# One-hots of the gate spreading: the first of each pair moved from VectorE and ScalarE to GpSimd

## The reference, cut to what matters

```python
best, sel = lax.top_k(cand, TOPK)
experts = jnp.take_along_axis(cand_idx, sel, axis=-1)
g = jax.nn.softmax(best, axis=-1).astype(tb.dtype)
act = jax.nn.gelu(jnp.einsum('td,thkd->thk', tb, u[experts]), approximate=False)
return jnp.einsum('thk,thkd->td', g * act, v[experts])
```

## Time and profile before

| | |
|---|---|
| median of 3 runs | 2717.73 us (2707.57 to 2720.52) |
| the profiled execution's own time | 2710.97 us |
| its span in the profile | 2709.1 us |
| its mean granted clock of TensorE | 0.979 |
| busy: PE, PEld | 2546.0 us (94%), 2100.2 us (78%) |
| busy: DVE, ACT, POOL | 1420.7 us (52%), 458.0 us (17%), 669.8 us (25%) |
| moved by DMA | 903.23 MB |

### The profile page before, as it was taken

The page is one execution under the profiler, slowest core; times in us unless marked ns, Lnnn a source line. Parts: engine busy times, 40 slices in busy tenths (PEclk is TensorE's granted clock), DMA queues, the critical chain, the costliest instruction groups (busy, mean ns, idle before and its releaser), DMA issues. The chain is left out here.

```text
span 2709.1 us, 40606 instructions
## 1 busy us (share of the span) xinstructions
PE 2546.0 (94%) x16083; PEld 2100.2 (78%) x16083; DVE 1420.7 (52%) x3161; ACT 458.0 (17%) x1371; POOL 669.8 (25%) x651
## 2 busy tenths in 40 slices
PE   8889987799899999999999999998999999999998
PEld 5564463346499999999999866464999999899997
DVE  2430020122279989985555321223799899855554
ACT  3220020012021125430000010121111254300000
POOL 0005000000004336563333000000043365633330
PEclk9799998999999999999999999999999999999999
DMA  7789969996928999999999896949089999999996
GB/s 244 239 280 295 350 246 386 407 362 248 407 85 315 382 353 396 402 384 410 409 409 409 295 378 223 379 162 368 1 339 376 350 397 401 385 409 409 409 409 226
DMA packets 254618, 903.23 MB, mean 333 GB/s; under 512 B 28522, under 2 KB 35850, under 8 KB 243631
## 3 DMA queue, kind: packets, MB, share of 16 engines
q1 hardware_dynamic: 170254, 608.05, 59.9%
q0 software_dynamic: 84176, 292.59, 28.0%
HBM read 880.10 MB, written 109.08 MB: 365 GB/s over the span
## 5 line engine op out<-in xcount | busy, mean ns | idle before, releaser
L2999 PE MATMUL ps<-xT,front 128*128 128x176 f32 x4096 | 645.1, 315 | 11.5 <-DMA front<-in_peer_uT 11.1
L2999 PEld LDWEIGHTS ps<-xT,front 128*128 128x128 f32 x4096 | 611.6, 190 | 29.5 <-DMA front<-in_peer_uT 28.2
L3032 PE MATMUL ps<-p1e_S,p_qT 128*128 128x192 f32 x2048 | 337.4, 327 | 6.5 <-DMA p_qT<-in_peer_v 6.5
L3032 PE MATMUL ps<-p0e_S,p_qT 128*128 128x192 f32 x2048 | 337.1, 327 | 4.8 <-DMA p_qT<-in_peer_v 4.8
L3032 PEld LDWEIGHTS ps<-p1e_S,p_qT 128*128 128x128 f32 x2048 | 332.4, 190 | 10.9 <-DMA p_qT<-in_peer_v 10.9
L3032 PEld LDWEIGHTS ps<-p0e_S,p_qT 128*128 128x128 f32 x2048 | 332.4, 190 | 8.9 <-DMA p_qT<-in_peer_v 8.6
L2735 DVE CUSTOM_DVE_ANT_0 front<-front,x_tok 128x1024 f32<-128x1024 f32 x256 | 308.6, 1218 | 10.2 <-DMA front<-in_peer_u,p1e_expert 4.1
L2636 POOL DMA_INDIRECT front<-in_peer_u,p0e_expert x128 | 158.3, 1237 | 340.8 <-DVE p0e_expert L2798 165.9
L2636 POOL DMA_INDIRECT front<-in_peer_u,p1e_expert x128 | 158.2, 1236 | 340.4 <-DVE p1e_expert L2798 163.8
L2745 DVE SCALAR_TENSOR_TENSOR h_tok<-front,p0e_dots,h_tok 128x1024 f32<-128x1024 f32 x127 | 163.1, 1284 | 145.6 <-DMA front<-in_peer_v,p0e_expert 144.8
L2745 DVE SCALAR_TENSOR_TENSOR h_tok<-front,p1e_dots,h_tok 128x1024 f32<-128x1024 f32 x127 | 163.1, 1284 | 144.0 <-DMA front<-in_peer_v,p1e_expert 143.2
(11 more groups left out here) (494 smaller groups left out, 2985.4 us busy)
## 6 DMA issues: line engine op xcount, KB each, us to landing
front<-in_peer_uT SPq DMA_DIRECT2D x256, 512.0 KB, 7.3
p_qT<-in_peer_v SPq DMA_DIRECT2D x256, 512.0 KB, 7.3
out_swa_sample<-in_cache_swa_w SPq DMA_DIRECT2D x32, 2040.0 KB, 23.8
e_ring<-in_mla_pages SPq DMA_DIRECT2D x84, 272.0 KB, 4.7
e_ring<-in_swa_kT SPq DMA_DIRECT2D x16, 1024.0 KB, 9.6
e_arena<-in_swa_v SPq DMA_DIRECT2D x16, 1024.0 KB, 14.3
out_swa_sample<-in_cache_swa_w SPq DMA_DIRECT2D x8, 2016.0 KB, 31.7
e_ring<-in_attn_w_in SPq DMA_DIRECT2D x6, 2048.0 KB, 35.1
```

The costliest lines, as they stand in the source:

```text
L2999: mm = pe.matmul(k.ps[:, SB[i % len(SB)], 0:TU], ur[:, i % NU, c, :], k.xT[:, c, D0:D0 + TU], start=(c == 0), stop=(c == KC - 1))
L3032: return pe.matmul(k.ps[:, c // 2, c % 2 * TD:(c % 2 + 1) * TD], vr[:, i % NV, c * P:(c + 1) * P], S[:, i, :], start=False, stop=(i == STE ...
```

## The change

GpSimd makes hotI, and puts the gate in at once: for each token of a group one `tensor_scalar` of 128x128 compares `iota` with the key (a scalar per partition) and multiplies by the gate (a second one). VectorE makes hotJ only; ScalarE's `gate_hots` is gone. GpSimd does the four instructions of group G ahead of gather `rows_behind_hots(G)`, five gathers further than VectorE's row at that point of its order; groups 0 and 1 both stand ahead of gather 62. The semaphore `keys_ready` is folded into `act_ready`, whose counts move up by two.

```diff
+    ROWS_AHEAD = 57
...
+        def rows_behind_hots(G):
+            return ROWS_AHEAD + sum(1 + i % 2 for i in range(FIRST - 1, SPLIT[max(G, 1) - 1] - 1)) + 5
...
         @block.gpsimd
         def _(pool):
+            def first_hots(G):
+                if G == 0:
+                    pool.wait_ge(act_ready, 5)
+                if G >= 2:
+                    pool.wait_ge(spread, G - 1)
+                if G == MORE_GROUP:
+                    pool.wait_ge(hot_ready, MORE_GROUP + 1)
+                for m in range(TG):
+                    t = TG * G + m
+                    last = pool.tensor_scalar(out=hotI[:, G % 2, m, :], in0=iota[:, :], scalar1=T3[:, 0, t:t + 1],
+                                              scalar2=T3[:, 2, t:t + 1], op0=ALU.is_equal, op1=ALU.mult)
+                last.then_inc(hot_turned, 1)
...
+                while G < GROUPS and rows_behind_hots(G) == n:
+                    first_hots(G)
+                    G += 1
                 if n >= NG:
                     pool.wait_ge(rows_used, n - NG + 1)
...
-                for hot, a in ((hotI, 0), (hotJ, 1)):
-                    dve.tensor_tensor(out=hot[:, G % 2, :, :], in0=iota[:, :].unsqueeze(1).to_broadcast([P, TG, P]),
-                                      in1=T3[:, a, t0:t0 + TG].unsqueeze(2).to_broadcast([P, TG, P]),
-                                      op=ALU.is_equal).then_inc(hot_ready, 1)
+                dve.tensor_tensor(out=hotJ[:, G % 2, :, :], in0=iota[:, :].unsqueeze(1).to_broadcast([P, TG, P]),
+                                  in1=T3[:, 1, t0:t0 + TG].unsqueeze(2).to_broadcast([P, TG, P]),
+                                  op=ALU.is_equal).then_inc(hot_ready, 1)
...
-            def gate_hots(G):
-                t0 = TG * G
-                act.wait_ge(hot_ready, 2 * G + 1)
-                for m in range(TG):
-                    last = act.activation(hotI[:, G % 2, m, :], hotI[:, G % 2, m, :], ACT.Copy,
-                                          scale=T3[:, 2, t0 + m:t0 + m + 1])
-                last.then_inc(hot_gated, 1)
...
-                pe.wait_ge(hot_ready, 2 * G + 2)
-                pe.wait_ge(hot_gated, G + 1)
+                pe.wait_ge(hot_ready, G + 1)
+                pe.wait_ge(hot_turned, G + 1)
```

More of the change, by code:

```diff
@@ L2518, in peer @@
         diff_ready, gated = k.sem(name + "_diff"), k.sem(name + "_gated")
-        turned, keys_ready = k.sem(name + "_turned"), k.sem(name + "_keys_ready")
+        turned, hot_turned = k.sem(name + "_turned"), k.sem(name + "_hot_turned")
         u_landed = [k.sem(f"{name}_u_landed{s}") for s in range(NU)]
@@ L2522, in peer @@
         dotted, gelu_done = k.sem(name + "_dotted"), k.sem(name + "_gelu")
-        hot_ready, hot_gated, spread = k.sem(name + "_hot"), k.sem(name + "_hot_gated"), k.sem(name + "_spread")
+        hot_ready, spread = k.sem(name + "_hot"), k.sem(name + "_spread")
         gate_copied, weight_ready, scaled = k.sem(name + "_copied"), k.sem(name + "_weight"), k.sem(name + "_scaled")
@@ L2597, in _ @@
                 if i == MORE_GELU_AT + NU:
-                    sp.wait_ge(act_ready, 4)
+                    sp.wait_ge(act_ready, 6)
                     sp.dma_start(carried[0:MORE, :], more_dots[:, :]).then_inc(more_landed, 16)
@@ L2625, in _ @@
         def _(pool):
+            def first_hots(G):
[10 more added lines that the diff above has]
+                last.then_inc(hot_turned, 1)
             pool.wait_ge(chosen, 1)
+            G = 0
             for n in range(ROWS):
@@ L2639, in _ @@
                 ).then_inc(row_landed[n % NG], 16)
+            assert G == GROUPS
         @block.vector
@@ L2783, in row @@
                     if col == 0:
-                        dve.wait_ge(act_ready, 5)
+                        dve.wait_ge(act_ready, 7)
                         link(dve.tensor_tensor(out=dots[:, :], in0=dots[:, :], in1=IJ[:, 0, 2, :], op=ALU.mult))
@@ L2815, in _ @@
             row()
-            dve.wait_ge(keys_ready, 2)
+            assert n_rows == ROWS_AHEAD
+            dve.wait_ge(act_ready, 5)
             one_hots(0)
@@ L2906, in take_keys @@
                                    k.ps[:, i, 0:3 * P].rearrange("p (a t) -> p a t", a=3)[:, :, 0:n],
-                                   ACT.Copy).then_inc(keys_ready, 1)
+                                   ACT.Copy).then_inc(act_ready, 1)
             before.root(act, 0)
@@ L2937, in _ @@
                 gelu(i)
-                if i == TURN_AT:
-                    gate_hots(0)
                 while G < groups_by(i):
@@ L2942, in _ @@
                     G += 1
-                    if G < GROUPS:
-                        gate_hots(G)
                 if i == MORE_GELU_AT:
```

## The result

The changed kernel takes 3037.38 us (median of 4 runs, 3033.85 to 3041.80) against 2716.89: a ratio of 1.118, 95% interval 1.116 to 1.120. That is 320 us slower, where 135 were forecast and the range ended at +237. The direction and the engine were right, the size was not.

The account below looks back on a forecast made before the run. VectorE was taken as full, with TensorE and the transfers level; afterwards GpSimd sets the pace. 46 groups x (5.34 - 3.87) = 67.6 us per layer, 135 for two, on 2717.7 gives 2853 us; range 2718 to 2955.

Parts of the forecast that it names:

- The bound: Gate spreading: three engines and the transfers level; what the stretch gains or loses goes to the end, once per layer.
- What goes: Per group VectorE loses one of two one-hots, 0.60 us, and ScalarE four gate multiplications of 0.390 us.
- The start's 2 us: Start of the spreading: three quick GpSimd steps fewer before the first spreading weights load may give 2 us.
- the rival in which GpSimd keeps up: Spreading: short tensor_scalars slip in and gathers wait less; gain about 10 to 14 us, 2704 to 2708; chance 0.17.
- What comes: Four new GpSimd tensor_scalars per group, priced from copies at 0.40 us each, bounds 0.28 and 0.55.
- the same sum: GpSimd's work plus waits per spreading group: 3.84 + 2.95 x 2.70/T, giving 5.34 us.
- T: New group period in the spreading, forecast at 5.34 us against 3.87 before.
- the sum of the upper bound: Spreading group with tensor_scalars of 0.55 and waits of 1.22: T = 4.44 + 4.81 x 2.70/T = 6.45, +237 us.
- The shared access: Spreading: GpSimd reads wait for VectorE instructions with two SBUF inputs, 0.41 or 0.60 us each times their share.
- Who waits: Spreading: GpSimd's gathers come late, VectorE waits for rows, TensorE for the weights and scalings behind them.
- VectorE and the clock: Spreading: VectorE not the bound at 4.87 us; rival, TensorE's clock falls, +343 us at the lower level, chance 0.04.

Follow-up runs that it names:

- v0_left_out: Changed kernel with GpSimd's four tensor_scalars and the first one-hot left out, only the semaphore raised: 2715.93 us, ratio 0.9994 to the kernel before.
- c2: Changed kernel with VectorE's row product replaced by a sum with one SBUF input: 2864.19 us.
- c1: Kernel before the change, with row products replaced by plain sums with one SBUF input: 2716.12 us.
- d1: Changed kernel with GpSimd's one-hots four gathers earlier in its order: 3001.39 us.
- the four kernels: Changed kernel with GpSimd's tensor_scalar at half the columns, compare only, constants for scalars, or two products: 2934.82, 2930.50, 2897.78, 2903.60 us.

## Why the prediction was wrong

- *The bound.* Right: three engines and the transfers level, the stretch going to the end once per layer, nothing made up later. The loss is 160 and 161 us.
- *What goes.* The start's 2 us and the 10 to 14 us of the rival in which GpSimd keeps up were too much: v0_left_out shows no gain (by its interval some 4 us at most).
- *What comes: the failed step.* "I take 0.40 us, between them, the copy being the nearer kind", with 0.55 as upper bound: it measured 0.79 us alone. The copy has no compare (0.35 us of it) and reads no scalars. With 0.79 in the same sum, T = 5.40 + 2.95 x 2.70/T = 6.6 us, or +252 us; this one term makes 117 of the 185 us missing. With 0.79 in the sum of the upper bound T is 7.20 us and the loss 306 us, so the measured 7.13 lies within it: the range failed by this price.
- *The shared access.* Its existence and the need for two SBUF inputs held (c2). Its size was low: 0.28 us per tensor_scalar was in the sum ((0.41 + 3 x 0.60) x 0.506/4), 0.47 is the mean, at a share of only 2.70/7.13 = 0.38: 1.24 us times the share, where the sum had 0.55 on average and the upper bound 1.02. Several waits in one instruction, which the bound left out, would explain that; they are not shown. The Trainium skill's rule (SBUF — State Buffer, Who interferes with whom) held for the tensor_scalars (mean 1.26 us beside row products, 0.82 beside sums with one input); that gathers wait too, c1's timeline shows again, 1.75 us behind one-hots for 0.94.
- *Who waits.* Wrong in place: VectorE stands before gates, TensorE before one-hots, not VectorE before rows. It would be rows with another order (d1).
- *VectorE and the clock.* VectorE has slack, as forecast. TensorE's granted clock fell to 0.85 and 0.88 in the stretches; its price stayed out, as argued: 230 us busy in 335, and GpSimd, the pace, waits for TensorE nowhere from 1040 to 1160 us.

## What to carry to other kernels

Before moving work off a full engine, leave it out on the chip once: here that showed a gain of nothing, whatever the new place costs. Price an instruction on another engine by its own operation, columns and scalars, not by a copy; if the trace has none, its upper bound is not twice the copy. And an engine's idle share is no room when each of its instructions has to wait for another engine's access. That the waits grow with an instruction's reads fits the four kernels; it is a reason to count them, not yet a rule.

## What the runs showed of the hardware

- GpSimd's tensor_scalar, 128 columns, compare and multiplication with two scalars per partition: 0.79 us alone. On VectorE the same takes 0.26 from start to start.
- Behind VectorE's two-input instructions it stood up to 2.6 us, past two boundaries between them; a gather in the earlier trace rows past none, one in c1_one_input_before (1041.15) past one. With constants in place of scalars it never stood more than 1.04 us.
- TensorE after an idle stretch of 3.5 us: eight spreading products in 2.05 us, against 1.13 after 1.7 us idle (the granted clock is 1.00 from 1104 to 1106 us and 0.50, the level of 1.2 GHz, from 1112 to 1114, by the last two lines, columns as in the earlier trace rows):
```profile
1104.00 1.13 PE L3032 MATMUL ps<-h_tok 128*128 128x128 f32 x8 [1.73 <-DVE h_tok L2774]
...
1111.03 2.05 PE L3032 MATMUL ps<-h_tok 128*128 128x128 f32 x8 [3.51 <-issue]
...
1104.00:1106.00 2.00, 2.00 (x15) 2.00 (x16) 0.48 (x2) 0.31 (x1) 1.63 (x2) 1.00 0.66 188
1112.00:1114.00 2.00, 2.00 (x10) 2.00 (x9) 0.54 (x2) 0.31 (x1) 1.96 (x4) 0.50 0.54 127
```
